# Dealing adjacent weight rows to partitions, so that expert weights come in 4 KB packets

## The chip, the core and the metric

The kernel runs on one core of a Trainium2 chip. The time is device microseconds of one execution. Before the change three runs gave 1325.62, 1323.4 and 1325.61 us, median 1325.61. The engines are TensorE (PE, matmuls; PEld are its weight loads), VectorE (DVE), ScalarE (ACT), GpSimd (POOL) and SyncE (SP), which here issues every DMA.

## The reference

One block of a diffusion backbone on 256 latent tokens with 256 context tokens, D = 2048, all in float32. Cut to what matters:

```python
mods_x = split((silu(c) @ w_mod + b_mod), 6)          # shift, scale, gate for attention; shift, scale, gate for ffn
nx = modulated_norm(h_x, attn_norm, sa_x, sca_x)       # rmsnorm * (1 + scale) + shift
... = split(nx @ w_in)                                 # latent attention (8 heads) and gated short convolution
h_new = h_x + ga_x * merge_head_groups(o_mla, o_conv)  # o @ w_out
# mixture of experts: 32 experts of width 256, 4 of them for each token, and a shared expert of width 512
idx, w = route(xf, w_router, bias)
g, u = xf @ w_exp_gate[e], xf @ w_exp_up[e]            # (2048, 256) each, for every expert e
routed = sum_e (silu(g) * u * comb[:, e]) @ w_exp_down[e]      # (256, 2048)
shared = (silu(xf @ w_sh_gate) * (xf @ w_sh_up)) @ w_sh_down
out = rmsnorm(h_new + gf_x * (routed + shared), final_norm)
```

where xf is the modulated norm of h_new with ffn_norm, shift sf_x and scale scf_x. A product over D sums 2048 rows, and the order of the rows is free as long as activations and weights agree on it.

## The kernel before, in words

The program is written out by hand, one instruction stream for each engine with semaphores between them. The order of work is the order of the code; only buffers that come free set when a DMA starts.

*Start (0 to about 83 us).* SyncE loads constants, x and ctx, then the first slices of w_mod (2 MB each), then w_in and more of w_mod. PE multiplies silu(c) with w_mod in groups of 512 columns. Groups 0 to 7 go through PE. For groups 8 and on VectorE accumulates w_mod rows (L1239) into the tile `part`, and PE only sums over partitions: `mod_sum_cols` (L508) takes 128 columns of `part` as weights and a column of ones as the moving side, four times for each group. It leaves one modulation value per partition. Groups 8 to 15 are the shift and scale of the ffn; they become `modT` and `amul2`.

*Attention and convolution (to about 574 us)*, then the ffn norm: VectorE (L1456) and ScalarE (L1082) write normalised rows `xh` from `xres`, one half of the tokens each, in four chunks of 512 columns. PE transposes them (L778) into `hT`, and router and shared expert follow.

*Experts.* `ring` holds the weights of one pair of experts: gate and up in four quarters of the 2048 rows (`gu`), down in two tiles. `load_quarter` (L404) issues four DMAs of 512 KB for a quarter, `load_down` (L411) one for each slice of 512 columns and each expert. Row 128 c + p of a weight lies on partition p, so a packet, the piece contiguous in HBM and in SBUF, has 256 numbers (1 KB) for gate and up and 512 (2 KB) for down. A pair has passes of 64 tokens for each expert. In a pass PE multiplies the gathered tokens with gate and up (L485, 64 matmuls as the trace counts them), gathers the tokens of the next pass with bf16 matmuls from three parts of `xh`, applies down, and scatters with `pickT`; VectorE adds (L1619). PE frees quarter q for SyncE with `gu_used[q]`, down with `down_used[n]`. There are 16 pairs and 17 passes. Code before and after the loop over pairs is separate code, and a pass that may be left out stands before each pass.

Of the kernel before, what the change touches and what calls it, by code (L numbers as in the profile page):

```python
# [9 lines left out]
ACT = mybir.ActivationFunctionType  # L10
# [5 lines left out]
P = 128  # L16
D = 2048
T = 256
KC = D // P
# [5 lines left out]
NE, NG, FF = 32, 4, 256  # L25
# [15 lines left out]
V_AN, V_QN, V_KN, V_CW, V_OM, V_OC, V_FN = 0, 16, 20, 22, 46, 54, 62  # L41
# [32 lines left out]
def block_kernel(nc, x, c, ctx_in, c_ctx, w_mod, b_mod, attn_norm, w_in, q_a_norm, w_q_b, kv_a_norm, w_kv_b,  # L74
                 conv_w, o_norm_mla, o_norm_conv, w_out, ffn_norm, w_router, router_bias,
                 w_exp_gate, w_exp_up, w_exp_down, w_sh_gate, w_sh_up, w_sh_down, final_norm, consts, out):
    with ExitStack() as stack:
        def sb(name, shape, dt=F32):
            return stack.enter_context(nc.sbuf_tensor(name, shape, dt))

        def sem(name):
            return stack.enter_context(nc.semaphore(name))


        xres = sb("xres", [P, 2, D])
# [6 lines left out]
        part = sb("part", [P, 2, 512])  # L92
        modT = sb("modT", [P, 96, 2])
# [8 lines left out]
        csil = sb("csil", [32, P])  # L102
        vecT = sb("vecT", [P, NVEC])
        bT = sb("bT", [P, 96])
        amul = sb("amul", [P, KC, 2])
        amul2 = sb("amul2", [P, KC])
        stat = sb("stat", [P, 16])
        wr = sb("wr", [P, KC, NE])
# [22 lines left out]
        xh = slot[3].rearrange("p (t d) -> p t d", t=2)  # L131

        gu = ring[:, 0:16384].rearrange("p (q u g k n) -> p q u g k n", q=4, u=2, g=2, k=4)
        down = [slot[4 + u].rearrange("p (k n) -> p k n", k=2) for u in range(2)]
# [85 lines left out]
        down_in = [sem(f"down_in{n}") for n in range(4)]  # L220
        down_used = [sem(f"down_used{n}") for n in range(4)]
# [3 lines left out]
        gu_full, silu_done, act_ready, actT_full, actT_out, dn_full, ye_out, sc_full, y_add = (  # L225
            sem("gu_full"), sem("silu_done"), sem("act_ready"), sem("actT_full"), sem("actT_out"), sem("dn_full"),
            sem("ye_out"), sem("sc_full"), sem("y_add"))
        mean_sq, root, mean_wide, root_wide = sem("mean_sq"), sem("root"), sem("mean_wide"), sem("root_wide")
        fin_h, fin_sq, fin_gain, fin_dve, fin_act, stored = (sem("fin_h"), sem("fin_sq"), sem("fin_gain"),
                                                             sem("fin_dve"), sem("fin_act"), sem("stored"))  # L230
# [5 lines left out]
        wq = w_q_b[0].rearrange("(c p) n -> p c n", p=P)  # L236
        wkv = w_kv_b[0].rearrange("(c p) n -> p c n", p=P)
        wo = w_out[0].rearrange("(c p) n -> p c n", p=P)
        wg = w_exp_gate[0].rearrange("e (c p) n -> p e c n", p=P)
        wu = w_exp_up[0].rearrange("e (c p) n -> p e c n", p=P)  # L240
        wd = w_exp_down[0].rearrange("e (c p) n -> p e c n", p=P)
        sg = w_sh_gate[0].rearrange("(c p) n -> p c n", p=P)
        su = w_sh_up[0].rearrange("(c p) n -> p c n", p=P)
        sd = w_sh_down[0].rearrange("(c p) n -> p c n", p=P)

        def k_of(s, k):
            return slot[s].rearrange("p (k n) -> p k n", k=k)

        FIRST = 0

# [17 lines left out]


        SH_SLOT = (0, 1, 2, 0, 4, 5)  # L270
        SH_USE = (11, 10, 11, 12, 1, 2)

        block = stack.enter_context(nc.Block())

# [2 lines left out]
        def _(sp):  # L277
# [77 lines left out]
            sp.dma_start(wr[:, :, :], w_router[0].rearrange("(c p) n -> p c n", p=P)).then_inc(router_in, 16)  # L355
            sp.dma_start(rb[:, :], router_bias.to_broadcast([P, NE])).then_inc(router_in, 16)


# [36 lines left out]
            sp.dma_start(k_of(2, KC), sg[:, :, FF:2 * FF]).then_inc(w_full[2], 16)  # L395
# [3 lines left out]
            sp.dma_start(k_of(0, KC), sg[:, :, 0:FF]).then_inc(w_full[0], 16)  # L399
            sp.dma_start(k_of(5, 2), sd[:, 2:4, :]).then_inc(w_full[5], 16)  # L400
            sp.wait_ge(sh_gate, 2)
            sp.dma_start(k_of(0, KC), su[:, :, FF:2 * FF]).then_inc(w_full[0], 16)


            def load_quarter(i, q):
                for u in range(2):
                    for g, src in ((0, wg), (1, wu)):
                        sp.dma_start(gu[:, q, u, g, :, :].rearrange("p k n -> p (k n)").rearrange("p (k n) -> p k n", k=4),
                                     src[:, bass.ds(2 * i + u, 1), 4 * q:4 * q + 4, :]
                                     .rearrange("p a c n -> p (a c) n")).then_inc(gu_in[q], 16)  # L410
# [12 lines left out]
            sp.wait_ge(sh_gate, 4)  # L423
            load_quarter(0, 2)
            sp.wait_ge(sh_down, 8)
            for n in range(4):
# [4 lines left out]
            for n in range(4):  # L431
                load_down(0, n, 1)
            with sp.Fori(1, NE // 2) as i:
                for q in range(4):
                    sp.wait_ge(gu_used[q], i)
                    load_quarter(i, q)
                for n in range(4):
# [45 lines left out]
        def _(pe):  # L483
            def mm(o, l, r, start, stop):
                return nc.tensor.matmul(o, l, r, start=start, stop=stop)  # L485
# [364 lines left out]
            def pair_pass(i, t, last, ahead=True):  # L850
# [27 lines left out]
                def scatter(n):  # L878
                    pe.wait_ge(ye_out, 4 * t + (n + 1))
                    for h in range(2):  # L880
                        m = 2 * n + h
                        pe.wait_ge(y_add, 8 * t + (16 + max(m - 1, 0)))
                        ins = mm(ps[:, 6 + h, :], pickT[:, 128 * h:128 * h + 128], ye[:, 512 * n:512 * n + 512], True, True)
                        if n < 3 and h == 0 and last:
                            ins.then_inc(down_used[n + 1], 1)
                    ins.then_inc(sc_full, 1)

                for n in range(4):
                    pe.wait_ge(down_in[n], 32 * i + 32)
                    if n >= 2:  # L890
                        pe.wait_ge(ye_out, 4 * t + (n - 1))
                    for k in range(2):
                        for u in range(2):
                            ins = mm(ps[64 * u:64 * u + 64, 4 + n % 2, :], actT[:, k, 64 * u:64 * u + 64],
                                     down[u][:, k, 512 * n:512 * n + 512], k == 0, k == 1)
                            if n == 1 and k == u == 0 and last:
                                ins.then_inc(down_used[0], 1)
                    ins.then_inc(dn_full, 1)
                    if n == 0:
                        pe.wait_ge(pickT_out, t + 1)  # L900
                    else:
                        scatter(n - 1)
# [23 lines left out]
        def _(sc):  # L926
# [251 lines left out]
        def _(ve):  # L1178
# [141 lines left out]
            with ve.Fori(0, 4) as i:  # L1320
# [21 lines left out]
                for m in range(2):  # L1342
# [4 lines left out]
            steps[0] += 4 * LINKS  # L1347

            ve.wait_ge(modT_done, 16)
            link(V.tensor_tensor(modT[:, 48:80, 0:1], modT[:, 48:80, 0:1], bT[:, 48:80].unsqueeze(2), ALU.add))  # L1350
            V.scalar_tensor_tensor(out=amul2[:, :].rearrange("p (c a) -> p c a", a=1), in0=modT[:, 64:80, 0:1], scalar=1.0,
                                   in1=vecT[:, V_FN:V_FN + KC].rearrange("p (c a) -> p c a", a=1),
                                   op0=ALU.add, op1=ALU.mult).then_inc(mods_ready, 1)


# [97 lines left out]
            ve.wait_ge(root, roots[0])  # L1453
            ve.wait_ge(mods_ready, 1)
            for n in range(4):
                V.tensor_scalar(xh[:, 0, 512 * n:512 * n + 512], xres[:, 0, 512 * n:512 * n + 512], stat[:, 10:11], None,  # L1456
                                ALU.mult).then_inc(xh_ready, 1)
# [236 lines left out]
```

## Time and profile before

| | |
|---|---|
| median of three runs | 1325.61 us |
| span of the profiled execution, first to last instruction | 1322.1 us |
| PE busy | 1222.6 us |
| DVE busy | 517.6 us |
| ACT busy | 227.0 us |
| DMA | 379.59 MB, mean 287 GB/s |
| packets | 276337, of them under 2 KB 182864 |

The profile is of one execution, whose own time is given by its span alone; the runs beside it are timed from outside. Busy shares are averages over stages. Idle time of an engine counts only where the chain that ended last runs through it.

### The profile page before, as it was taken

Reading aid. Unit: us, or ns where it says so; the run is one execution under the profiler, and the core shown is the slowest. Engines: PE = TensorE matmul, PEld = TensorE weight load, DVE = VectorE, ACT = ScalarE, POOL = GpSimd, SP = SyncE. Lnnn points to the kernel's source line nnn. Section 1 sums busy time; section 2 is a strip of 40 time slices with the busy share of each in tenths; the row PEclk is TensorE's granted clock in tenths of the full one; section 3 lists DMA queues with packets and bytes.
Section 4 is the critical chain, followed back from the end, with each engine's and each line's share of the span. In section 5 each row is a group of like instructions: output and inputs, shape, how many; then the busy total and the mean of one; then the engine's idle time right before and its main releaser. Section 6 shows DMA issues by size and latency. Waiting matters only on the chain.

```text
span 1322.1 us, 16803 instructions
## 1 busy us (share of the span) xinstructions
PE 1222.6 (92%) x6125; PEld 655.8 (50%) x6126; DVE 517.6 (39%) x1058; ACT 227.0 (17%) x482; POOL 8.7 (1%) x13
## 2 busy tenths in 40 slices
PE   2789999999999899989979999999999999999974
PEld 0435588888744544457834444444334444444421
DVE  1200487656267588542532222222223332222215
ACT  4210200000125400040011111111111111111103
POOL 0000000000000000000000000000000000000001
PEclk9989999999999999989989999999999999999988
DMA  9999989996574499763549999945999999999951
GB/s 341 345 354 335 315 297 366 350 326 219 163 278 141 151 343 387 274 243 128 181 145 361 344 344 345 347 156 162 348 348 346 350 349 357 343 345 346 347 198 63
DMA packets 276337, 379.59 MB, mean 287 GB/s; under 512 B 12674, under 2 KB 182864, under 8 KB 274640
## 3 DMA queue, kind: packets, MB, share of 16 engines
q1 hardware_dynamic: 276304, 379.14, 84.1%
q8 instruction: 22, 0.36, 0.1%
q14 instruction: 11, 0.09, 0.0%
HBM read 377.01 MB, written 2.10 MB: 287 GB/s over the span
## 4 chain that ended last, share of the span: by engine, by line
PE 88%; DVE 3%; DMA 3%; issue 2%; SPq 2%; ACT 1%; POOL 0%; POOLq 0%; DVEq 0%; ACTq 0%
PE ps L485 85%; DMA ring<-in_w_mod 3%; DVE nreg L1619 1%; PE ps L855 1%; SPq L311 1%; PE ps L778 0%; SPq L303 0%; DVE tiny L1386 0%; PE ps L555 0%; DVE nreg L1623 0%; PE ps L730 0%; PE ps L872 0%; ACT nreg L928 0%; PE ps L500 0%; ACT nreg L1049 0%
## 5 line engine op out<-in xcount | busy, mean ns | idle before, releaser
L485 PE MATMUL ps<-nreg,ring 128*128 128x256 f32 (+1 forms) x1280 | 301.0, 395 | 10.2 <-ACT nreg L928 5.8
L485 PEld LDWEIGHTS ps<-nreg,ring 128*128 128x128 f32 x1280 | 244.0, 192 | 63.9 <-issue 21.8
L485 PE MATMUL ps<-ring,nreg 128*64 128x512 f32 x1088 | 241.2, 602 | 0.0
L1239 DVE SCALAR_TENSOR_TENSOR part<-ring,csT,part 128x512 f32<-128x512 f32 x240 | 180.4, 752 | 9.2
L1619 DVE TENSOR_TENSOR nreg<-nreg,ps 128x512 f32<-128x512 f32 x136 | 87.4, 684 | 176.2 <-PE ps L485 176.2
L485 PEld LDWEIGHTS ps<-ring,nreg 128*64 128x64 f32 x1088 | 77.5, 139 | 151.9 <-issue 151.9
L485 PE MATMUL ps<-nreg,conv 128*128 128x512 f32 x272 | 134.9, 618 | 13.5 <-DVE nreg L1619 13.5
L485 PE MATMUL ps<-ring,conv 128*64 128x512 f32 x544 | 128.0, 602 | 0.5 <-ACT conv L928 0.5
L485 PE MATMUL ps<-ring 128*128 128x512 f32 x256 | 110.8, 592 | 0.0
L485 PEld LDWEIGHTS ps<-nreg,conv 128*128 128x128 f32 x272 | 46.0, 189 | 101.5 <-DVE nreg L1619 60.2
L485 PE MATMUL ps<-pick,qnT 128*128 128x128 bf16 x544 | 93.2, 220 | 1.1 <-issue 0.6
L928 ACT ACTIVATE nreg<-ps 128x512 f32<-128x512 f32 (+1 forms) x104 | 57.7, 555 | 208.6 <-PE ps L485 195.7
L485 PE MATMUL ps<-pick,kq 128*128 128x128 bf16 x544 | 92.9, 219 | 0.0
L485 PE MATMUL ps<-pick,hb 128*128 128x128 bf16 x544 | 92.9, 219 | 0.0
L485 PEld LDWEIGHTS ps<-ring 128*128 128x128 f32 x256 | 48.6, 190 | 60.4 <-issue 60.3
L1611 DVE TENSOR_TENSOR conv<-ps,conv 128x256 f32<-128x256 f32 x17 | 7.2, 425 | 178.9 <-ACT conv L1124 178.9
L485 PEld LDWEIGHTS ps<-ring,conv 128*64 128x64 f32 x544 | 34.5, 136 | 76.7 <-issue 74.3
L1600 DVE TENSOR_SCALAR nreg<-ps,amul,modT 128x128 f32<-128x128 f32 x136 | 46.5, 405 | 63.9 <-PE ps L485 63.9
L1116 ACT ACTIVATE nreg<-ps,modT,amul 128x128 f32<-128x128 f32 x136 | 51.2, 456 | 66.0 <-PE ps L485 66.0
L485 PEld LDWEIGHTS ps<-pick,qnT 128*128 128x128 bf16 x544 | 53.1, 98 | 18.5 <-issue 14.2
L928 ACT ACTIVATE conv<-ps 128x256 f32<-128x256 f32 x42 | 16.2, 385 | 228.2 <-PE ps L485 139.4
L485 PE MATMUL ps<-ring,csT 128*32 128x512 f32 x256 | 33.7, 655 | 23.3 <-DMA ring<-in_w_mod 23.3
(193 smaller groups left out, 753.1 us busy)
## 6 DMA issues: line engine op xcount, KB each, us to landing
ring<-in_w_mod SPq DMA_DIRECT2D x88, 1024.0 KB, 9.4
ring<-in_w_exp_gate SPq DMA_DIRECT2D x128, 512.0 KB, 8.2
ring<-in_w_exp_up SPq DMA_DIRECT2D x128, 512.0 KB, 8.6
ring<-in_w_exp_down SPq DMA_DIRECT2D x128, 512.0 KB, 8.6
ring<-in_w_in SPq DMA_DIRECT2D x15, 2048.0 KB, 11.9
ring<-in_w_out SPq DMA_DIRECT2D x8, 2048.0 KB, 10.9
ring<-in_w_mod SPq DMA_DIRECT2D x4, 2048.0 KB, 19.8
ring<-in_w_sh_up SPq DMA_DIRECT2D x2, 2048.0 KB, 10.2
```

The lines of the kernel that those rows point to most:

```text
L311: sp.dma_start(slots_[q], wm[:, 4 * q:4 * q + 4, bass.ds(g * 512, 512)]).then_inc(m_full[q], 16)
L485: return nc.tensor.matmul(o, l, r, start=start, stop=stop)
L855: ins = nc.tensor.transpose(ps[:, 3, 128 * j:128 * j + 128], pickw[:, j, :], ident)
L928: return nc.scalar.activation(o, i_, ACT.Copy)
L1116: ins = nc.scalar.activation(xg[:, k, :], ps[:, b % 2, 128 * j:128 * j + 128], ACT.Identity, bias=modT[:, 3 * KC + k, 0:1], scale=amul2[:, ...
L1239: ins = V.scalar_tensor_tensor(out=acc, in0=w, scalar=scale, in1=acc, op0=ALU.mult, op1=ALU.add)
L1600: ins = V.tensor_scalar(xg[:, k, :], ps[:, b % 2, 128 * j:128 * j + 128], amul2[:, k:k + 1], modT[:, 3 * KC + k, 0:1], ALU.mult, ALU.add)
L1611: V.tensor_tensor(act[:, 1, :], ps[:, 2, FF:2 * FF], act[:, 0, :], ALU.mult).then_inc(act_ready, 1)
L1619: V.tensor_tensor(yacc[:, h, cols], yacc[:, h, cols], ps[:, 6 + h, :], ALU.add).then_inc(y_add, 1)
```

## The change

Rows of gate and up are dealt anew: partition p takes rows 512 q + 4 p + j for quarter q and j = 0 to 3. Its four rows lie side by side in HBM, 4 KB in one packet. The router's weights are dealt likewise, and the shared expert's gate and up too; since these are loaded by halves of their columns, their packets stay 1 KB, and each load becomes four DMAs. Down is loaded in two halves of 1024 columns (4 KB packets) instead of four slices, with two semaphores instead of four.

The activations have to be dealt alike. `xh` is written so that its chunk 4 q + j holds columns 512 q + 4 c + j: the two norm writers read `xres` with a step of four elements and write without gaps. The modulation sums take every fourth column of `part`. Bias and gain in that order are loaded by three new DMAs with 16-byte pieces.

```diff
+            for at, src in ((bT2[:, 0:KC], b_mod[0, 3 * D:4 * D]), (bT2[:, KC:2 * KC], b_mod[0, 4 * D:5 * D]),
+                            (fnT[:, :], ffn_norm[0])):
+                sp.dma_start(at.rearrange("p (q j) -> p q j", q=4), src.rearrange("(q p j) -> p q j", q=4, j=4))\
+                  .then_inc(cols_in, 16)
             sp.wait_ge(mod_rows, 1)
...
-        wg = w_exp_gate[0].rearrange("e (c p) n -> p e c n", p=P)
+        wg = w_exp_gate[0].rearrange("e (q p j) n -> p e q (j n)", q=4, j=4)
-        sg = w_sh_gate[0].rearrange("(c p) n -> p c n", p=P)
+        sg = w_sh_gate[0].rearrange("(q p j) n -> p q j n", q=4, j=4)
...
+        def by_row(v, n):
+            return v.rearrange("p (j c) -> p j c", c=n)
+        def by_col(v):
+            return v.rearrange("p (c j) -> p j c", j=4)
...
-            sp.dma_start(k_of(1, KC), su[:, :, 0:FF]).then_inc(w_full[1], 16)
+            def load_shared(s, src, half):
+                for q in range(4):
+                    sp.dma_start(k_of(s, KC)[:, 4 * q:4 * q + 4, :], src[:, q, :, FF * half:FF * half + FF])\
+                      .then_inc(w_full[s], 16)
+            load_shared(1, su, 0)
...
-                sp.dma_start(down[u][:, :, 512 * n:512 * n + 512],
-                             wd[:, bass.ds(2 * i + u, 1), :, 512 * n:512 * n + 512]
+                sp.dma_start(down[u][:, :, 1024 * n:1024 * n + 1024],
+                             wd[:, bass.ds(2 * i + u, 1), :, 1024 * n:1024 * n + 1024]
...
-                    ins = mm(ps[:, 5, j:j + 1], part[:, b, 128 * j:128 * j + 128], ones[:, 0:1], True, True)
+                    ins = mm(ps[:, 5, j:j + 1], part[:, b, :].rearrange("p (c j) -> p j c", j=4)[:, j, :], ones[:, 0:1],
+                             True, True)
...
-                        if n < 3 and h == 0 and last:
-                            ins.then_inc(down_used[n + 1], 1)
+                        if n in (0, 2) and h == 0 and last:
+                            ins.then_inc(down_used[n // 2], 1)
...
-                            if n == 1 and k == u == 0 and last:
-                                ins.then_inc(down_used[0], 1)
...
-                nc.scalar.activation(xh[:, 1, 512 * n:512 * n + 512], xres[:, 1, 512 * n:512 * n + 512], ACT.Identity,
-                                     scale=stat[:, 11:12]).then_inc(xh_act, 1)
+                nc.scalar.activation(by_row(xh[:, 1, 512 * n:512 * n + 512], 128), by_col(xres[:, 1, 512 * n:512 * n + 512]),
+                                     ACT.Identity, scale=stat[:, 11:12]).then_inc(xh_act, 1)
```

VectorE's norm writer (L1456) changes in the same way, and `modT` and `amul2` are built from `bT2` and `fnT` behind a wait on `cols_in`.

On SyncE, at the start of the program, this stands before:

```order
L291 DMA ring<-in_ctx 128x2x2048
L295 DMA ring<-in_w_mod 128x8x512 x4
L300 DMA ring<-in_w_in 128x16x256 x2
L302 DMA ring<-in_w_in 128x16x256
L303 DMA kq<-in_w_in 128x16x64
```

and this after the change (`bT` is the order's name for bT2):

```order
L300 DMA ring<-in_ctx 128x2x2048
L304 DMA ring<-in_w_mod 128x8x512 x4
L309 DMA bT<-in_b_mod 128x4x4 x2
L309 DMA fnT<-in_ffn_norm 128x4x4
L313 DMA ring<-in_w_in 128x16x256 x2
L315 DMA ring<-in_w_in 128x16x256
L316 DMA kq<-in_w_in 128x16x64
```

Three DMAs of 16-byte pieces have come in between w_mod and w_in.

On SyncE, at the end of one turn of the loop over pairs, before (L414 is the line of `load_down`; ISA is a wait; `128x2x512 x2` is one slice for two experts):

```order
L408 DMA ring<-in_w_exp_gate 128x4x256
L408 DMA ring<-in_w_exp_up 128x4x256
L414 DMA ring<-in_w_exp_down 128x2x512 x2
L414 ISA
L414 DMA ring<-in_w_exp_down 128x2x512
```

and after:

```order
L427 DMA ring<-in_w_exp_gate 128x1024
L427 DMA ring<-in_w_exp_up 128x1024
L432 DMA ring<-in_w_exp_down 128x2x1024 x2
L432 ISA
L432 DMA ring<-in_w_exp_down 128x2x1024
```

The order of gate, up and down is unchanged; a piece of gate and up is one row of 1024 numbers, and down goes out in four DMAs of a turn and not eight.

## Rows read from the trace of the kernel before

**Rows 1.** The cores: span, and mean granted clock of TensorE.
```profile
core 0: 1322.1 us, clock 0.980
```

**Rows 2.** The page: busy us (share, instructions); DMA queue (packets, MB, share).
```profile
PE 1222.6 (92%) x6125; PEld 655.8 (50%) x6126; DVE 517.6 (39%) x1058; ACT 227.0 (17%) x482; POOL 8.7 (1%) x13
...
q1 hardware_dynamic: 276304, 379.14, 84.1%
```

**Rows 3.** Waits of PE, whole span: releaser, us in total, times, longest.
```profile
PE ps L485 <- DMA ring<-in_w_mod: 23.3, 7, 15.2
...
PE ps L485 <- DMA ring<-in_w_in: 1.9, 1, 1.9
```

**Rows 4.** Chain of waits, end of the start: start us, us, what.
```profile
73.52 9.74 DMA ring<-in_w_mod
```

**Rows 5.** Waits of PE from 700 to 1300 us, all of them.
```profile
PE ps L485 <- DVE nreg L1619: 12.5, 16, 0.8
PE ps L855 <- issue: 6.0, 2, 5.8
PE ps L872 <- DVE conv L1611: 0.9, 1, 0.9
PE ps L485 <- ACT conv L928: 0.5, 1, 0.5
```

**Rows 6.** Chain of waits, first matmuls of two successive passes.
```profile
904.87 16.67 PE ps L485 x112
...
941.04 16.67 PE ps L485 x112
```

**Rows 7.** Stretches of one pass: busy, clock, DMA share, GB/s last.
```profile
953.00:957.00 4.00, 4.00 (x49) 2.58 (x46) 0.42 (x1) 0.97 (x3) 0.00 (x0) 1.00 1.10 348
...
973.00:977.00 4.00, 3.12 (x9) 0.93 (x7) 1.59 (x3) 0.00 (x0) 0.00 (x0) 1.00 1.06 388
```

**Rows 8.** Waits of SyncE's queue, 904 to 1270 us.
```profile
SPq L408 <- PE ps L485: 110.5, 20, 42.1
```

**Rows 9.** Chain of waits, the two longest pieces of issue.
```profile
678.95 6.83 issue
...
1265.79 5.82 issue
```

**Rows 10.** DMA queues, 1265 to 1272 us: packets, MB, share.
```profile
q1 hardware_dynamic: 1097, 2.10, 81.4%
q8 instruction: 1, 0.02, 1.0%
```

**Rows 11.** Stretches at the second stall, columns as in rows 7.
```profile
1269.00:1270.00 1.00, 0.00 (x0) 0.00 (x0) 0.00 (x0) 0.00 (x0) 0.00 (x0) 1.00 0.98 373
1270.00:1271.00 1.00, 0.00 (x0) 0.00 (x0) 0.00 (x0) 0.00 (x0) 0.00 (x0) 0.52 0.39 135
```

**Rows 12.** Timeline of PE, gate and up matmuls of two passes.
```profile
940.97 13.96 PE L485 MATMUL ps<-ring,nreg 128*64 128x512 f32 x64
...
1272.22 16.24 PE L485 MATMUL ps<-ring,nreg 128*64 128x512 f32 x64
```

**Rows 13.** Stretches at the start, columns as in rows 7.
```profile
52.00:56.00 4.00, 4.00 (x20) 3.54 (x19) 0.00 (x0) 0.00 (x0) 0.00 (x0) 1.00 1.10 348
56.00:60.00 4.00, 2.11 (x9) 1.18 (x8) 0.00 (x0) 0.00 (x0) 0.00 (x0) 1.00 1.05 206
```

**Rows 14.** Timeline: weight loads of one column sum.
```profile
188.00 1.08 PEld L485 LDWEIGHTS ps<-cst,part 128*128 128x128 f32 x8
```

**Rows 15.** Timeline: norm writers and transposes.
```profile
577.92 2.56 ACT L1082 ACTIVATE ring<-xres,stat 128x512 f32<-128x512 f32 x4 [1.21 <-POOL stat L467]
577.92 1.68 DVE L1456 TENSOR_SCALAR ring<-xres,stat 128x512 f32<-128x512 f32 x4 [0.82 <-POOL stat L467]
...
578.78 6.21 PE L778 MATMUL ps<-cst,ring 128*128 128x128 f32 x32 [4.83 <-ACT ring L1082]
```

**Rows 16.** Timeline: down loads of the loop's last turn, third scatter.
```profile
1254.49 8.77 SPq L414 DMA_DIRECT2D ring<-in_w_exp_down  x8
...
1261.04 1.98 PE L485 MATMUL ps<-nreg,conv 128*128 128x512 f32 x4
```

More of the change, by code:

```diff
@@ L104, in block_kernel @@
         bT = sb("bT", [P, 96])
+        bT2 = sb("bT2", [P, 2 * KC])
+        fnT = sb("fnT", [P, KC])
         amul = sb("amul", [P, KC, 2])
@@ L219, in block_kernel @@
         gu_used = [sem(f"gu_used{q}") for q in range(4)]
-        down_in = [sem(f"down_in{n}") for n in range(4)]
-        down_used = [sem(f"down_used{n}") for n in range(4)]
+        down_in = [sem(f"down_in{n}") for n in range(2)]
+        down_used = [sem(f"down_used{n}") for n in range(2)]
         pick_ready, pickw_ready, gx_full, gx_act, gx_dve, pickT_full, pickT_out = (
@@ L227, in block_kernel @@
             sem("ye_out"), sem("sc_full"), sem("y_add"))
+        cols_in = sem("cols_in")
         mean_sq, root, mean_wide, root_wide = sem("mean_sq"), sem("root"), sem("mean_wide"), sem("root_wide")
@@ L238, in block_kernel @@
         wo = w_out[0].rearrange("(c p) n -> p c n", p=P)
-        wg = w_exp_gate[0].rearrange("e (c p) n -> p e c n", p=P)
-        wu = w_exp_up[0].rearrange("e (c p) n -> p e c n", p=P)
+        wg = w_exp_gate[0].rearrange("e (q p j) n -> p e q (j n)", q=4, j=4)
+        wu = w_exp_up[0].rearrange("e (q p j) n -> p e q (j n)", q=4, j=4)
         wd = w_exp_down[0].rearrange("e (c p) n -> p e c n", p=P)
-        sg = w_sh_gate[0].rearrange("(c p) n -> p c n", p=P)
-        su = w_sh_up[0].rearrange("(c p) n -> p c n", p=P)
+        sg = w_sh_gate[0].rearrange("(q p j) n -> p q j n", q=4, j=4)
+        su = w_sh_up[0].rearrange("(q p j) n -> p q j n", q=4, j=4)
         sd = w_sh_down[0].rearrange("(c p) n -> p c n", p=P)
@@ L270, in block_kernel @@
         SH_SLOT = (0, 1, 2, 0, 4, 5)
-        SH_USE = (11, 10, 11, 12, 1, 2)
+        SH_USE = (14, 13, 14, 18, 1, 2)
         block = stack.enter_context(nc.Block())
@@ L354, in _ @@
             sp.dma_start(k_of(2, 2), wkv).then_inc(w_full[2], 16)
-            sp.dma_start(wr[:, :, :], w_router[0].rearrange("(c p) n -> p c n", p=P)).then_inc(router_in, 16)
+            sp.dma_start(wr[:, :, :].rearrange("p (q j) n -> p q (j n)", q=4),
+                         w_router[0].rearrange("(q p j) n -> p q (j n)", q=4, j=4)).then_inc(router_in, 16)
             sp.dma_start(rb[:, :], router_bias.to_broadcast([P, NE])).then_inc(router_in, 16)
@@ L392, in _ @@
             sp.wait_ge(wo_full, 3)
-            sp.dma_start(k_of(1, KC), su[:, :, 0:FF]).then_inc(w_full[1], 16)
+            def load_shared(s, src, half):
[3 more added lines that the diff above has]
+            load_shared(1, su, 0)
             sp.wait_ge(wo_half, 4)
-            sp.dma_start(k_of(2, KC), sg[:, :, FF:2 * FF]).then_inc(w_full[2], 16)
+            load_shared(2, sg, 1)
             sp.wait_ge(acc_done, 16 * 16)
@@ L398, in _ @@
             sp.wait_ge(wo_full, 4)
-            sp.dma_start(k_of(0, KC), sg[:, :, 0:FF]).then_inc(w_full[0], 16)
+            load_shared(0, sg, 0)
             sp.dma_start(k_of(5, 2), sd[:, 2:4, :]).then_inc(w_full[5], 16)
             sp.wait_ge(sh_gate, 2)
-            sp.dma_start(k_of(0, KC), su[:, :, FF:2 * FF]).then_inc(w_full[0], 16)
+            load_shared(0, su, 1)
             def load_quarter(i, q):
@@ L407, in load_quarter @@
                     for g, src in ((0, wg), (1, wu)):
-                        sp.dma_start(gu[:, q, u, g, :, :].rearrange("p k n -> p (k n)").rearrange("p (k n) -> p k n", k=4),
-                                     src[:, bass.ds(2 * i + u, 1), 4 * q:4 * q + 4, :]
-                                     .rearrange("p a c n -> p (a c) n")).then_inc(gu_in[q], 16)
+                        sp.dma_start(gu[:, q, u, g, :, :].rearrange("p k n -> p (k n)"),
+                                     src[:, bass.ds(2 * i + u, 1), q, :].rearrange("p a x -> p (a x)")).then_inc(gu_in[q], 16)
             def load_down(i, n, u):
-                sp.dma_start(down[u][:, :, 512 * n:512 * n + 512],
-                             wd[:, bass.ds(2 * i + u, 1), :, 512 * n:512 * n + 512]
+                sp.dma_start(down[u][:, :, 1024 * n:1024 * n + 1024],
+                             wd[:, bass.ds(2 * i + u, 1), :, 1024 * n:1024 * n + 1024]
                              .rearrange("p a c n -> p (a c) n")).then_inc(down_in[n], 16)
@@ L425, in _ @@
             sp.wait_ge(sh_down, 8)
-            for n in range(4):
+            for n in range(2):
                 load_down(0, n, 0)
@@ L430, in _ @@
             sp.wait_ge(sh_down, 16)
-            for n in range(4):
+            for n in range(2):
                 load_down(0, n, 1)
@@ L436, in _ @@
                     load_quarter(i, q)
-                for n in range(4):
+                for n in range(2):
                     sp.wait_ge(down_used[n], i)
@@ L883, in scatter @@
                         ins = mm(ps[:, 6 + h, :], pickT[:, 128 * h:128 * h + 128], ye[:, 512 * n:512 * n + 512], True, True)
-                        if n < 3 and h == 0 and last:
-                            ins.then_inc(down_used[n + 1], 1)
+                        if n in (0, 2) and h == 0 and last:
+                            ins.then_inc(down_used[n // 2], 1)
                     ins.then_inc(sc_full, 1)
                 for n in range(4):
-                    pe.wait_ge(down_in[n], 32 * i + 32)
+                    if n % 2 == 0:
+                        pe.wait_ge(down_in[n // 2], 32 * i + 32)
                     if n >= 2:
@@ L1349, in _ @@
             ve.wait_ge(modT_done, 16)
-            link(V.tensor_tensor(modT[:, 48:80, 0:1], modT[:, 48:80, 0:1], bT[:, 48:80].unsqueeze(2), ALU.add))
+            ve.wait_ge(cols_in, 48)
+            link(V.tensor_tensor(modT[:, 48:80, 0:1], modT[:, 48:80, 0:1], bT2[:, :].unsqueeze(2), ALU.add))
             V.scalar_tensor_tensor(out=amul2[:, :].rearrange("p (c a) -> p c a", a=1), in0=modT[:, 64:80, 0:1], scalar=1.0,
-                                   in1=vecT[:, V_FN:V_FN + KC].rearrange("p (c a) -> p c a", a=1),
+                                   in1=fnT[:, :].rearrange("p (c a) -> p c a", a=1),
                                    op0=ALU.add, op1=ALU.mult).then_inc(mods_ready, 1)
@@ L1455, in _ @@
             for n in range(4):
-                V.tensor_scalar(xh[:, 0, 512 * n:512 * n + 512], xres[:, 0, 512 * n:512 * n + 512], stat[:, 10:11], None,
-                                ALU.mult).then_inc(xh_ready, 1)
+                V.tensor_scalar(by_row(xh[:, 0, 512 * n:512 * n + 512], 128), by_col(xres[:, 0, 512 * n:512 * n + 512]),
+                                stat[:, 10:11], None, ALU.mult).then_inc(xh_ready, 1)
             gate_out(OUT_GROUP + 3)
```

## The prediction

> **What bounds the kernel now.** I began with the cores and the busy shares: one core, a mean granted clock of 0.980 [rows 1], TensorE (PE) busy 92% of 1322.1 us and the DMA queue 84% [rows 2]. Both are near full, so either could be the limit, and the list of TensorE's waits has to decide. It says [rows 3] that PE waited 25.2 us for weights by DMA (23.3 for w_mod, 1.9 for w_in). The chain of waits, in order of time, has the last of it at 73.52 to 83.3 us [rows 4]; from there the chain runs through PE. In the stretch 700 to 1300 us, where the expert weights are used, no DMA ends a wait of PE: the list has four rows [rows 5], 12.5 us behind VectorE's adds, 6.0 us of "issue" and crumbs.
>
> The chain also gives the beat of one expert pair, 904.87 to 941.04 us, 36.2 us [rows 6]. The bytes of one pair are 24 loads of 512 KB, 12.6 MB: 8.4 MB of gate and up in 1 KB packets at 348 GB/s, 24.1 us, and 4.2 MB of down in 2 KB packets at 388, 10.8 us [rows 7], together 34.9. So DMA fills its beat almost as PE does, but the one who waits is SyncE, 110.5 us for PE's release of gate and up buffers [rows 8], and not PE. A quarter is loaded when PE frees it and read one beat later. In this stretch faster packets shorten transfers that nobody waits for, and I cost the gain at nothing. PE's 36.2 us are the cover; transfers would have to get slower, not faster, to show.
>
> **Where DMA is on the path.** Two places are left. First the start, up to 83 us. Secondly, two stalls of PE that the chain calls "issue", at 678.95 us (6.83 us) and 1265.79 us (5.82 us) [rows 9]. Both stand where PE goes from one piece of program to another, into the pair loop and out of it. The DMA listing of the second has one packet of the instruction queue beside 2.10 MB of weights [rows 10]. Weights flow at 373 GB/s until 1270, at 135 in the next microsecond, and PE goes on at 1271.6 [rows 9, 11]. I read this as the program's fetch standing behind queued weight packets, which is an inference. After the stall the granted clock is 0.52 and less, TensorE's lower level (1.2 GHz) [rows 11], and the 64 gate and up matmuls of the last pass take 16.24 us against 13.96 in a pass at full clock [rows 12]: 2.3 us more.
>
> **The change part by part.**
> 1. *Start.* Three DMAs go in front of the first w_in load, 512 packets each of 16 bytes, 1536 in all. DMA is the limit there, so they are paid in full. The nearest row is the load of wkr, 2048 packets of 256 bytes: from 56 to 60 us DMA moved 206 GB/s where it had moved 348 before [rows 13]. 4 x 142 = 568 KB are lost, 1.6 us, and its own 0.52 MB cost 1.5 us more. For each packet that is 0.8 ns lost, or 1.5 ns with the payload: 1536 x 0.8 = 1.2 us, 1536 x 1.5 = 2.3 us. I take 1.8; ends 0 (if they slip into slack) and +5 (if 16 bytes are far worse than 256). The Trainium skill, "DMA: Bandwidth & Descriptors", Specifications, says that a transfer below 512 B is a read-modify-write; the wkr row has such packets too and would already carry that price.
> 2. *Column sums of the modulation.* Eight groups (n = 8 to 15) now give PE its weights from part with a step of four elements, 16 bytes. Before, the 8 weight loads of one sum take 1.08 us [rows 14], and eight sums 8.6 us, on PE's chain and hidden by nothing. No row shows a PE read with such a step. If it costs nothing, 0; if each load takes twice its time, +8.6 us. A gain is excluded, since the instructions are as many. I take 0: these fp32 loads need 0.13 us for 128 columns, a slow pace already, and fetching may not be what sets it. The upper end is rival B.
> 3. *Normalised rows.* Eight instructions now read xres with a 16-byte step. VectorE's four take 1.68 us and ScalarE's four 2.56 us, and PE, which waited 4.83 us for the first, then needs 6.21 us for 32 transposes [rows 15]. Only the first pair is ahead of PE; the others come every 0.64 us while PE takes 1.55 us for each. VectorE's 0.42 us may grow to ScalarE's 0.64 without being seen. If ScalarE's doubles, PE starts 0.6 to 0.7 us later. I take +0.4, ends 0 and +1.4 (both engines also hand back the transposes, later by as much).
> 4. *Shared expert, router, cols_in.* Four loads for one, with the same 1 KB packets: SyncE has nine more issues, among waits for PE. PE waited for none of these loads [rows 3, 5], nor for the router's, whose packets get longer. The wait on cols_in stands at the end of the convolution stage, far behind its loads. 0 for all.
> 5. *Expert loads.* I take 400 GB/s for 4 KB packets, an estimate a little above the 388 of 2 KB. Two releases of down stand for four. SyncE's first down load now waits for the first scatter; in the last turn SyncE comes to down only at 1254.49 us, about when that scatter is under way. The second waits for the third scatter, which starts at 1261.04 [rows 16], as the last load does now. 0 on the path.
> 6. *The two stalls.* At the second, the last 2.1 MB of down are released at 1262 us, 1 us into the third scatter. With 1 us to start and 5.2 us at 400 GB/s they end at 1268.3, where now the flow ends near 1270.4 [rows 11]. The stall shrinks by 2.1 us, from 5.8 to 3.7. The clock may then stay up or not: half of 2.3, 1.1 us. At the first stall the 2.1 MB of down in flight should end 1 us sooner (0.6 us by rate alone, 388 to 400 and a quicker start): 1.0. Together -4.2 us, ends 0 and -7.
>
> Sum: 1.8 + 0 + 0.4 + 0 + 0 - 4.2 = -2.0 us. The profiled execution has a span of 1322.1 us and the runs' median is 1325.61, so 3.5 us lie around the span or between executions. 1325.6 - 2.0 = 1323.6 us.
>
> **Rivals.**
> A, the forecast: no large term, 1323.6 us, own range 1320.5 to 1327. Chance 0.48.
> B, strided weight loads cost. Each of the 64 load records takes up to twice its time, +4 to +8.6 us: 1328 to 1332. For it: nothing covers them, the matmul beside each has one column. Against: the loads are slow already. It decides from +0.07 us a load (4.5 us, which outweighs the stalls). Chance 0.22. The Trainium skill, "SBUF — State Buffer", in "Door 1: The DMA port swizzle", speaks for it: reads want at least two hits in each 16-byte line, and a step of four fp32 has one. By that rule the loads, and the eight instructions of point 3, slow down. No row of before shows such a read, and the page gives no size.
> C, the 16-byte packets cost 5 us: 1325.6 + 5 + 0.4 - 4.2 = 1327 us. For it, they are 16 times smaller than wkr's; against, they carry next to no bytes. Chance 0.08.
> D, both stalls shrink by their upper end and the clock is kept: -7, so 1325.6 + 1.2 - 7 = 1320 us. For it are the rates in the stall; against, down's last half is still released as late. Chance 0.18.
> E, DMA sets the beat after all, and 16 pairs gain 1 us or more, to 1308 us. Against it is the list of waits, with not one DMA row. Chance 0.04.
>
> **How the numbers follow.** 0.2% is 2.65 us, about what runs of this kernel can tell from no change (its three runs span 2.2 us). Faster, below 1322.9: 0.15 of A, all of D and E, 0.37. Slower, above 1328.3: 0.01 of A, 0.2 of B and 0.04 of C, 0.25. Same: 0.38. The range for 8 in 10 reaches from 1319, a little beyond D, to 1330, the middle of B.
>
> **What would show it.** Right: the beat of a pair stays 36.2 us while DMA moves 400 GB/s in it, with pauses between; the last wait for w_mod, at 73 to 83 us, ends 1 to 2 us later; the 8 loads on part still take 1.08 us; the stall near 1266 us is 2 us shorter. Wrong: another beat than 36.2 us (E, or contention that I have not seen), 2 us for 8 loads on part (B), a start later by 4 us or more (C), or stalls as long as before although the transfers end sooner, which would refute my reading of them.

## The result, and the profile after

The changed kernel is slower: 1335.49 us median (1334.11 to 1336.61, 4 runs) against 1325.06 (1323.4 to 1325.62, 4 runs), a ratio of 1.0082 with a 95% interval of 1.0067 to 1.0096. The forecast was 1323.6, range 1319 to 1330; the time lies above that range, and above the 1328 to 1332 us of rival B too. The cost of rival B came true (6.9 us, of 4 to 8.6), but it is not the whole. The profiled execution has a span of 1334.3 us, 12.2 more than the one of before. It is among the slower ones of its four, and some of the 12.2 us is where the clock happened to fall.

The page first: busy time, and the DMA queue (packets, MB, share).

```profile
span 1334.3 us, 16601 instructions
...
PE 1231.7 (92%) x6125; PEld 664.2 (50%) x6126; DVE 518.2 (39%) x1058; ACT 228.3 (17%) x482; POOL 8.7 (1%) x13
...
q1 hardware_dynamic: 160832, 379.16, 78.3%
```

Beside [rows 2], the bytes are the same and the packets are 160832 instead of 276304; the queue's share fell from 84.1 to 78.3%. So the change does what it says to DMA. PE has as many instructions and 9.1 us more of them, PEld 8.4 us more.

The chain of waits (start us, us, what) gives the account by places. These are the end of the start, the convolution stage, the first stall and two successive passes.

```profile
73.48 11.22 DMA ring<-in_w_mod
84.74 1.98 PE ps L503 x8
...
88.50 15.25 PE ps L503 x64
...
162.72 236.46 PE ps L503 x1052
...
688.53 7.43 issue
...
915.83 16.67 PE ps L503 x112
...
951.99 16.67 PE ps L503 x112
...
1276.88 7.32 issue
```

| stretch | before | after | more |
|---|---|---|---|
| to the end of the last w_mod wait | 83.3 | 84.7 | 1.4 |
| from there to the convolution stage | 75.5 | 78.0 | 2.5 |
| convolution stage, unbroken on PE | 229.5 | 236.5 | 6.9 |
| from its end to the output projection | 68.6 | 66.8 | -1.8 |
| from there to the router's matmuls (the norm lies in it) | 128.1 | 128.6 | 0.5 |
| first stall | 6.83 [rows 9] | 7.43 | 0.6 |
| from its end to the second stall | 580.0 | 580.9 | 0.9 |
| of this, beat of a pair | 36.17 [rows 6] | 36.16 | 0 |
| second stall | 5.82 [rows 9] | 7.32 | 1.5 |
| behind it | 50.5 | 50.1 | -0.4 |

From the router's matmuls to the first stall it is 94.0 us in either. Leaving out the beat, the lines add up to the 12.2 us but for rounding. The second line is the clock: the 8 matmuls behind the last wait take 1.98 us instead of 1.11 and the next 64 take 15.25 instead of 14.09, since PE's clock is at its lower level there (0.50 from 84 to 88 us in the table of stretches, 1.00 before). The line of -1.8 us is the clock as well: the same 203 matmuls, at a mean granted clock of 0.95 before and 0.97 after. Of the 0.9 us between the stalls, 112 matmuls behind the first stall account for all (19.20 us against 18.33), again at a low clock. The beat is the main thing that the change is about, and it has not moved. DMA in the pairs is as foreseen, as these stretches of the pass at 915.83 show (columns as in rows 7).

```profile
918.00:922.00 4.00, 4.00 (x22) 1.39 (x20) 1.83 (x8) 0.00 (x0) 0.00 (x0) 1.00 0.30 100
922.00:926.00 4.00, 4.00 (x20) 1.29 (x18) 0.00 (x0) 0.00 (x0) 0.00 (x0) 1.00 1.02 398
926.00:930.00 4.00, 4.00 (x25) 1.36 (x22) 0.00 (x0) 0.24 (x1) 0.00 (x0) 1.00 1.01 408
```

Gate and up flow at 398 to 408 GB/s where [rows 7] show 348, and there is now a pause (100 GB/s) in which nothing has been released. PE is as busy as ever. SyncE's wait for PE's releases (line, releaser, us, times, longest) has grown:

```profile
SPq L432 <- PE ps L503: 150.1, 20, 8.4
SPq L427 <- PE ps L503: 141.0, 40, 42.1
```

That is 291 us over 915 to 1281 us. Before, [rows 8] had 110.5 for gate and up, and down had 34.4. The growth is some 14 us a beat, and the transfers got only some 3 us shorter (12.6 MB at about 400 GB/s, an estimate, against 34.9 us). The rest was spent in issuing: before, once a few loads were under way, an issue of gate or up took 1.2 to 1.7 us, and in this pass each takes 0.33 to 0.39 (timelines of SyncE's queue). Both times stand in the same place, off PE's path.

The convolution stage grows by the weight loads of the column sums. Timeline of PEld, one sum:

```profile
191.93 1.94 PEld L503 LDWEIGHTS ps<-cst,part 128*128 128x128 f32 x8
```

1.94 us stands against 1.08 in [rows 14], 0.86 more, eight times: 6.9 us, the whole growth of the stage. Of one load the median is 329 ns and was 192 (loads overlap, so eight take less than eight times that).

### The profile page after: what moved, and what is told of

The parts are those of the page before. It is cut to its first block, busy times and chain, and to the rows that moved or that the text cites. A ratio compares the mean times of both kernels' runs of the same rounds, so it can differ in the third digit from the quotient of the medians.

```text
span 1334.3 us, 16601 instructions
## 1 busy us (share of the span) xinstructions
PE 1231.7 (92%) x6125; PEld 664.2 (50%) x6126; DVE 518.2 (39%) x1058; ACT 228.3 (17%) x482; POOL 8.7 (1%) x13
## 3 DMA queue, kind: packets, MB, share of 16 engines
q1 hardware_dynamic: 160832, 379.16, 78.3%
## 4 chain that ended last, share of the span: by engine, by line
PE 88%; DMA 3%; DVE 3%; issue 2%; ACT 2%; SPq 1%; POOL 0%; POOLq 0%; DVEq 0%; ACTq 0%
PE ps L503 85%; DMA ring<-in_w_mod 3%; DVE nreg L1638 1%; PE ps L574 1%; PE ps L874 1%; SPq L324 1%; SPq L316 0%; DVE tiny L1405 0%; DVE nreg L1642 0%; ACT ring L1100 0%; PE ps L518 0%; PE ps L749 0%; PE ps L891 0%; ACT nreg L946 0%; ACT nreg L1067 0%
```

## The experiments

### The strided weight loads, undone

```diff
-                    ins = mm(ps[:, 5, j:j + 1], part[:, b, :].rearrange("p (c j) -> p j c", j=4)[:, j, :], ones[:, 0:1],
-                             True, True)
+                    ins = mm(ps[:, 5, j:j + 1], part[:, b, 128 * j:128 * j + 128], ones[:, 0:1], True, True)
```

> The changed kernel, with the column sums of the modulation taken from part in contiguous pieces of 128 columns again (this leaves out the dealing of the modulation values, so they stand in the wrong order; no amount of work changes). In the changed kernel the median weight load on part is 329 ns against 192 before, and the chain of PE from 162.72 to 399.21 us is 236.5 us long against 229.5. Theory (strided weight loads are the main cost): loads back to 192 ns, that stretch back to 229.5 us, and the run 6.9 us faster than the changed kernel, about 1328.5 us. Rival (the stretch is longer for another reason, for instance packets of other sizes beside it): loads short, but the stretch stays near 236 us and the run near 1335 us.

1328.07 us (10 runs), ratio to before 1.0018 (1.0006 to 1.0029). The loads on `part` (min/median/max ns of a load) and the chain:

```profile
L503 PEld LDWEIGHTS ps<-cst,part x68: 186/192/192, 191.9 to 590.5; 128*128 128x128 f32 x68
```
```profile
162.70 229.53 PE ps L503 x1052
```

The stage is back at 229.53 us and the run 7.4 us faster than the changed kernel. The start stayed as in the changed kernel (162.70), so nothing there helped. Of the 10.4 us this is about two thirds, shown by taking it out. The firm figure is the 6.93 us of the stage; the ten times reach from 1324.62 to 1329.53 us, so the 7.4 is good to a microsecond or two.

### A step of two elements

On the kernel before, the loads take every second column:

```diff
-                    ins = mm(ps[:, 5, j:j + 1], part[:, b, 128 * j:128 * j + 128], ones[:, 0:1], True, True)
+                    ins = mm(ps[:, 5, j:j + 1], part[:, b, 256 * (j // 2):256 * (j // 2) + 256].rearrange("p (c j) -> p j c", j=2)[:, j % 2, :],
+                             ones[:, 0:1], True, True)
```

> The kernel before, with the weight loads of the column sums taking every second column of part (8 bytes apart) where the changed kernel takes every fourth (16 bytes). Order of the modulation values is not kept. Theory (a load is slowed once each element lies in a 16-byte line of its own): at two elements to a line the loads stay at 192 ns and the time at 1325 us. Rival (any step above one element slows the read): loads of 230 to 330 ns, and +2 to +7 us.

```profile
L485 PEld LDWEIGHTS ps<-cst,part x68: 186/196/197, 188.2 to 588.3; 128*128 128x128 f32 x68
```

196 ns and not 192, 1324.89 us, and the stage 229.87 us. A step of 8 bytes costs 2%, one of 16 bytes 71%. The Trainium skill, "SBUF — State Buffer", in "Door 1: The DMA port swizzle", says that at least two hits in each 16-byte line are needed for full bandwidth. The trace agrees (196 ns with two hits in a line, 329 ns with one), and it adds the size. Steps of 12 bytes and above 16 were not tried on PE, so that the 16-byte line is the reason, and not the length of the step, is the page's word and not shown.

### The 16-byte pieces, loaded later

```diff
-            for at, src in ((bT2[:, 0:KC], b_mod[0, 3 * D:4 * D]), (bT2[:, KC:2 * KC], b_mod[0, 4 * D:5 * D]),
...
             sp.wait_ge(mod_rows, 1)
...
+            for at, src in ((bT2[:, 0:KC], b_mod[0, 3 * D:4 * D]), (bT2[:, KC:2 * KC], b_mod[0, 4 * D:5 * D]),
...
             for s in range(2):
                 sp.wait_ge(conv_full, 20 + 2 * s)
```

> The changed kernel, with the three DMAs of 16-byte pieces issued behind the convolution loop instead of in front of the first w_in load. Theory (they delay the start by DMA time alone, 1.4 us, and the rest of the 3.9 us at the start is the granted clock, which falls at other moments): the last w_mod wait ends at 83.3 us again instead of 84.7, the run is 1.4 us faster than the changed kernel, give or take 2 us of clock, so 1332 to 1335 us. Rival (the pieces cost the whole 3.9 us, in SyncE's queue, where their issue took 11 us): 3.9 us faster, 1331.5 us, in every run.

The first place is in front of the first w_in load, the second behind the convolution loop. 1333.31 us (4 runs), ratio 1.0065 (1.0048 to 1.0082), 2.2 us below the changed kernel; the two intervals overlap (1.0067 to 1.0096 there), so this difference is not clear of noise. The chain at the end of the start:

```profile
73.69 9.56 DMA ring<-in_w_mod
83.29 1.11 PE ps L503 x8
...
85.72 14.09 PE ps L503 x64
...
158.90 236.46 PE ps L503 x1052
```

The wait ends at 83.25 us again, and the 2.5 us of slow clock behind it are gone too, in this execution. What the pieces do is seen in the timeline of SyncE's queue in the changed kernel:

```profile
24.73 8.29 SPq L309 DMA_DIRECT2D bT<-in_b_mod  x2
33.06 2.67 SPq L309 DMA_DIRECT2D fnT<-in_ffn_norm  x1
35.77 4.54 SPq L313 DMA_DIRECT2D ring<-in_w_in  x2
```

Their issue holds SyncE for 11 us, but the w_in loads behind them, issued at 35.77 us and not 30.5, still arrive in time to keep DMA busy. Hence 1.4 us of delay and not 11. The same three DMAs in this run, issued behind the convolution loop, take 1.4 us:

```profile
309.32 0.93 SPq L360 DMA_DIRECT2D bT<-in_b_mod  x2
310.30 0.51 SPq L360 DMA_DIRECT2D fnT<-in_ffn_norm  x1
```

DMA is as busy at either place (386 and 389 GB/s), but at the start four loads of 2 MB have been issued just ahead of them and here four of 1 MB. So the 11 us are not the price of the pieces; that they are the time in which a full queue drains is my reading.

The 2.2 us of the medians lie between my expectation (1.4) and the rival's 3.9. The other profiles part the two costs. With the pieces in front the last w_mod wait ends at 84.70, 84.51 and 84.03 us (the changed kernel, the run with contiguous column sums, and the first run of the next section), without them at 83.21 to 83.54 in nine profiles: 0.5 to 1.5 us are theirs. The clock is not tied to them. In the third of these three it is up again by 80 us and the convolution stage starts at 159.63 us, 0.8 later than before; and in the packets-only run below, without any such pieces, it is low at this place, and the stage starts at 162.00 us.

### The norm writers: stride on the other side, and alone

First, in the changed kernel, reading without gaps and writing with a step of 128 elements:

```diff
+        def to_rows(v):
+            return v.rearrange("p (j c) -> p c j", j=4)
...
+        def as_cols(v):
+            return v.rearrange("p (c j) -> p c j", j=4)
...
-                nc.scalar.activation(by_row(xh[:, 1, 512 * n:512 * n + 512], 128), by_col(xres[:, 1, 512 * n:512 * n + 512]),
+                nc.scalar.activation(to_rows(xh[:, 1, 512 * n:512 * n + 512]), as_cols(xres[:, 1, 512 * n:512 * n + 512]),
```

> The changed kernel, with the eight norm instructions reading xres without gaps and writing xh with a step of 128 elements, where the changed kernel reads with a step of four and writes without gaps; the result is the same tile. In the changed kernel ScalarE's four take 4.59 us against 2.56 before. Theory (the strided read is what costs): ScalarE back to 2.6 us for four, and the transposes start 0.5 us sooner. Rival (any stride on either side costs as much): 4.6 us again, or more, since the step is 512 bytes.

Then, in the kernel before, the dealt form alone (the same two views as in the change).

> The kernel before, with the eight norm instructions alone in their dealt form (reading xres with a step of four). The router then meets rows in the wrong order, so the number of passes in the expert stage may differ, and only the norm stage is to be read. Theory: ScalarE's four take 4.6 us, VectorE's four 2.5 us, and the stretch from the first of them to the router's matmuls grows by 0.5 to 0.6 us over the 7.0 us of before (577.92 to 584.92). Rival (the cost was in the changed kernel's surroundings): 7.0 us again.

Timeline of the three, ScalarE, VectorE and PE. The changed kernel:

```profile
586.95 4.59 ACT L1100 ACTIVATE ring<-xres,stat 128x512 f32<-128x512 f32 x4 [1.21 <-POOL stat L485]
586.95 2.47 DVE L1475 TENSOR_SCALAR ring<-xres,stat 128x512 f32<-128x512 f32 x4 [0.81 <-POOL stat L485]
...
594.49 1.93 PE L503 MATMUL ps<-nreg,wr 128*32 128x256 f32 x32
```

With the step on the writing side:

```profile
585.67 4.46 ACT L1106 ACTIVATE ring<-xres,stat 128x512 f32<-128x512 f32 x4 [1.21 <-POOL stat L491]
585.67 2.59 DVE L1481 TENSOR_SCALAR ring<-xres,stat 128x512 f32<-128x512 f32 x4 [0.81 <-POOL stat L491]
```

In the kernel before, alone:

```profile
576.44 4.58 ACT L1082 ACTIVATE ring<-xres,stat 128x512 f32<-128x512 f32 x4 [1.21 <-POOL stat L467]
...
584.02 1.93 PE L485 MATMUL ps<-nreg,wr 128*32 128x256 f32 x32
```

Against 2.56 and 1.68 us in [rows 15] both engines lose, ScalarE 80% and VectorE about 47%. My theory that only the read costs fell: the form that writes with a step of 512 bytes costs as much. Its two views also run over four elements at a time and not over 128, and no run parts this from the step. The stretch to the router's matmuls is 7.58 us alone and 7.54 in the changed kernel, where it was 7.0, so +0.5 us; close to the prediction's 0.4. The single times, 1332.88 and 1322.56 us, say no more than that nothing large hangs on it.

### The packets alone

In the kernel before, only the expert loads are changed (gate and up in rows of 4 KB, down in halves); the activations are not dealt to match.

```diff
-        wg = w_exp_gate[0].rearrange("e (c p) n -> p e c n", p=P)
+        wg = w_exp_gate[0].rearrange("e (q p j) n -> p e q (j n)", q=4, j=4)
...
-                sp.dma_start(down[u][:, :, 512 * n:512 * n + 512],
+                sp.dma_start(down[u][:, :, 1024 * n:1024 * n + 1024],
```

> The kernel before, with every expert load in 4 KB packets (gate, up and down as in the changed kernel), and nothing else of the change: activations are not dealt, so gate and up meet rows in the wrong order. Theory (the expert stage is bound by PE, so packets alone are worth nothing but what they do to the two stalls): beat of a pair 36.2 us, stalls of about 7.3 and 6.7 us as with down in halves, the run within 2 us of before, 1323 to 1326 us. Rival (larger packets do help or hurt PE in the pairs): a beat that differs by more than 0.1 us, the run over 2 us away.

1326.06 us (11 runs), ratio 1.0004 (0.9995 to 1.0013): no difference that can be measured. Its chain:

```profile
680.51 7.47 issue
...
762.38 16.67 PE ps L484 x112
...
798.52 16.67 PE ps L484 x112
...
1267.75 6.61 issue
```

The beat is 36.14 us. The gain that the packets might bring, 348 to 400 GB/s, is off the critical path. The two stalls are longer than before (7.47 and 6.61 us). To part down from gate and up, down alone in halves (the second edit above without the first, with two semaphores as in the change):

> The kernel before, with only down changed: two halves of 1024 columns with 4 KB packets and two semaphores, the rest as before. In the changed kernel the second stall is 6.7 to 7.3 us against 5.8 before, though down is the only load in flight there. Theory (down's first half is released later and so more of it is still on its way): the stall is 6.7 us or more here too. Rival (it comes from the packets of gate and up, or from chance): 5.8 us. Beat of a pair 36.2 us in either case.

Its stalls are 7.33 and 6.79 us. The three profiles with down in slices and weights in flight have 6.58 to 6.83 and 5.80 to 5.84 us, the seven with down in halves 7.19 to 7.47 and 6.61 to 7.32, so it is down's halves that lengthen them, by 0.4 to 0.9 us at the first and mostly 0.8 to 1.0 at the second; the 7.32 of the changed kernel is the longest of its kind. The first half waits for the first scatter, and then comes in pieces of 1 MB; which of the two does it is not shown. The one time was 1322.37 us, below the median of before: in its profile the stretch between the convolution stage and the output projection takes 66.7 us and not 68.6 (388.37 to 455.05 us, 388.33 to 456.94 before), with the same instructions, and more of the slow clock falls into the longer stalls themselves (the matmuls behind the first take 17.92 us, 18.33 before). One run cannot price the stalls.

### The two stalls

This is the kernel before with down loads kept out of the way:

```diff
             sp.wait_ge(sh_down, 16)
+            sp.wait_ge(pickT_full, 1)
             for n in range(4):
                 load_down(0, n, 1)
-            with sp.Fori(1, NE // 2) as i:
+            with sp.Fori(1, NE // 2 - 1) as i:
...
+            i = NE // 2 - 1
+            for q in range(4):
+                sp.wait_ge(gu_used[q], i)
+                load_quarter(i, q)
+            sp.wait_ge(gu_used[0], NE // 2)
+            for n in range(4):
+                sp.wait_ge(down_used[n], i)
+                for u in range(2):
+                    load_down(i, n, u)
```

> The kernel before, with down loads moved out of the way of the two stalls: the second expert's down of pair 0 is issued only once PE has started the pair code, and the down of the last pair only once PE has used the first gate and up quarter of that pair. Same work, same packets. Theory (the program's fetch stands behind queued weight packets): the stalls of 6.8 and 5.8 us shrink to 3 to 4 us each, the clock mostly stays up behind them, and the run is 5 to 9 us faster than before, 1316 to 1320 us. Rival (the fetch takes that long by itself, or is asked for late): stalls of 5.8 us or more again, and 1325 us.

1317.13 us (4 runs, 1316.72 to 1317.98), ratio 0.9949 (0.9933 to 0.9966): 7.2 us faster than before, and the fastest of all kernels here. Its chain:

```profile
679.07 4.17 issue
...
1263.42 3.07 issue
1266.94 15.55 PE ps L494 x64
```

6.83 and 5.82 us have become 4.17 and 3.07, with no weights in flight; the stretches of both show 0 to 16 GB/s. That is 5.4 us. The matmuls behind them are 1.0 us faster too, 17.97 and 15.55 us against 18.33 and 16.20 before, since less of them falls under the low clock; the two profiled spans differ by 6.0 us in all. So weights in flight lengthen the stalls, and the reading in the prediction holds that far: the program's fetch stands behind weight packets. But 3 to 4 us stay without any.

The packet of the instruction queue shows where the time goes. In slices of 0.1 us its place in each stall can be seen:

| profile | stalls | packet, us after PE stopped | PE goes on, us after the packet |
|---|---|---|---|
| before | 6.83, 5.82 | 4.2, 3.1 | 2.6, 2.7 |
| down in halves | 7.33, 6.79 | 4.7, 4.1 | 2.6, 2.7 |
| changed kernel | 7.43, 7.32 | 4.8, 4.8 | 2.6, 2.5 |
| this run | 4.17, 3.07 | 1.6, 0.5 | 2.6, 2.6 |

The time behind the packet is 2.5 to 2.9 us in all 24 stalls of the twelve profiles, whatever flows; weights in flight lengthen only the time up to it, by 2.6 us at either stall here. PE does not wait for the flow to end: at the second stall of before the packet passes at 1268.9 us, while DMA moves 403 GB/s and goes on at 373 in the next microsecond [rows 11].

### All mends together, and one that did not mend

VectorE deals while it accumulates, so that PE's loads are contiguous again, and the 16-byte pieces are late:

```diff
-                acc = part[:, b, :]
+                acc = by_row(part[:, b, :], 128) if dealt else part[:, b, :]
...
+                        if dealt:
+                            w = by_col(w)
...
```

> The changed kernel with VectorE dealing the columns while it accumulates and with the 16-byte pieces loaded behind the convolution loop, stalls as they are. Loads on part 192 ns; the accumulating instructions, 752 ns before, stay below 900 ns if VectorE is slowed by the step as little as its norm writer (0.42 to 0.62 us), and their pace stays off PE's path: PE's stretch 229.5 us, the run 1326 us (1335.5 - 6.9 - 2.2). Rival (a strided read slows VectorE's two-operand form as well and the accumulation becomes the bound in the convolution stage): over 1 us an instruction, PE waiting for VectorE there, and 1330 us or more.

1333.28 us (4 runs), ratio 1.0078 (1.0061 to 1.0095), where I had expected 1326. That is the 1333.31 of the run with late pieces alone, so taking the step away from PE brought nothing. The rival was right. VectorE's group in the convolution stage (busy us, mean ns), and the head of the chain there, 158 to 210 us:

```profile
L1258 DVE SCALAR_TENSOR_TENSOR part<-ring,csT,part 128x512 f32<-128x512 f32 x135 | 148.6, 1101 | 4.7
```
```profile
by line: DVE part L1258 62.4%; issue 8.0%; PE ps L503 6.5%; DVE kq L1214 6.5%; DVE qkv L1328 2.6%; DVE part L1255 2.5%; DVE conv L1356 2.2%; DVE conv L1348 1.4%; DVE qkv L1313 1.4%; DVE qkv L1334 1.4%; DVE kq L1209 1.2%; ACT kq L1004 1.2%; 
```

The mean of 1101 ns has some undealt instructions in it; from 167 to 202 us, where all are dealt, it is 1144. That instead of 752 ns makes VectorE the bound at the start of the stage, where PE had hidden it. The cost went from one engine to another.

The same with the late down loads:

> The changed kernel with all mends together: VectorE deals the columns while it accumulates (it reads w_mod with a step of four and writes part in contiguous pieces), so that PE's loads are contiguous; the 16-byte pieces are loaded behind the convolution loop; down loads stay out of the way of the two stalls as in the run on the kernel before. By the theory of the stalls: 1317 to 1321 us, faster than before, with nothing of it owed to 4 KB packets. Rival (stalls unchanged): 1326 us.

1325.68 us (8 runs), ratio 1.0016 (1.0005 to 1.0028). Its stalls are 4.00 and 3.04 us. It is 7.6 us below the run above, as on the kernel before (7.2), so the mend of the stalls works on either; but the whole missed its 1317 to 1321 by VectorE's loss.

## Why the prediction was wrong

1. *What bounds the kernel: right.* No DMA ends a wait of PE in the pairs, and faster packets are worth nothing there (ratio 1.0004 for the packets alone).
2. *The column sums: the first of two steps that failed.* The prediction took 0 between ends of 0 and +8.6 us, "these fp32 loads need 0.13 us for 128 columns, a slow pace already, and fetching may not be what sets it". They took +6.9 us, 1.94 us for 8 instead of 1.08. Pace told nothing of slack: no row showed how much of it was fetching, and the one rule at hand spoke for the cost. I had it as rival B with a chance of 0.22. With the right value the sum would have been 1330.5, still 5 us short: the other step is in point 5.
3. *The start: size about right, clock missed.* 1.8 us taken, 1.4, 1.3 and 0.8 measured at the last w_mod wait in three profiles. In the profiled execution a low clock made 2.5 us more of it; the medians put the whole at 2.2, with noise of that size. The rows of before show this place at full clock, and the prediction said nothing of the clock here.
4. *The norm: right*, 0.4 taken, 0.5 measured. VectorE's 0.42 us grew to 0.62, as allowed for, and ScalarE's 0.64 to 1.15, just short of the doubling that I had priced at 0.6 to 0.7.
5. *The stalls: the second step that failed, and about as large.* I took -4.2 us. They grew by 0.6 and 1.5 us, and the slower clock behind them cost 0.5 more, where 1.1 of gain stood in the 4.2. The prediction let the stall end 1.2 us behind the end of the flow, and the flow end 2.1 us sooner, at 400 GB/s after a start of 1 us. Neither came. The flow did not end sooner: the run with down in halves kept 344 to 426 GB/s for five microseconds around PE's stop, and still 1.68 MB came behind the stop (1.78 before). In the changed kernel it was slower, 164 to 336 GB/s at 1274 to 1279 us, and faded at 1281, 4 us into the stall:

```profile
1274.00:1275.00 1.00, 0.22 (x2) 0.11 (x1) 0.85 (x2) 0.00 (x0) 0.00 (x0) 1.00 0.69 164
...
1278.00:1279.00 1.00, 0.00 (x0) 0.00 (x0) 0.20 (x1) 0.00 (x0) 0.00 (x0) 1.00 0.95 336
...
1280.00:1281.00 1.00, 0.00 (x0) 0.00 (x0) 0.00 (x0) 0.00 (x0) 0.00 (x0) 1.00 0.52 205
```

   (Stretches of 1 us, changed kernel.) And the end of the flow is not what PE waits for: PE goes on 2.5 to 2.9 us behind the instruction packet, which passed 3.1 us after PE's stop before the change, 4.1 with down in halves and 4.8 in the changed kernel. That the fetch stands behind weights was right; its time was tied to the wrong event. Why the packet passes later with down in halves is open.

The account in medians: 10.4 us = 7.4 for the strided loads (taken out), 2.2 for the 16-byte pieces (taken out, not clear of noise), and 0.8 left for the norm and the stalls. That is less than those two show in the profile (0.5 and 2.1), by no more than the clock moves one stretch from one execution to the next (66.8 or 68.6 us from the convolution stage to the output projection). Only the first of the three is firm.

## What to carry to other kernels

Dealing a weight's rows to get longer packets has to be paid by whoever makes the activations match, and a step of 16 bytes in fp32 is not free on any of the three engines; look for that bill first, above all where the strided operand is a weight load that nothing covers. Before wanting faster transfers, see who waits: if SyncE waits for releases and no DMA ends a wait of PE, the packets are worth nothing. And where the chain shows "issue" at the door of a loop with weights in flight, move those weights: here that gave 7.2 us with no change of work, while 3 to 4 us of each stall stayed.

## What the runs showed that I had not expected

- The step's price for each element read: PE 137 ns for 128 (1.07 ns), ScalarE about 0.5 us for 512 (1.0 ns), VectorE 392 ns for 512 in the two-operand form (0.77 ns) and about 0.2 us for 512 in the one-operand form (0.4 ns). On PE's path the loads overlap, and 0.86 us for eight is 108 ns a load. With a step of 8 bytes PE pays 4 ns for 128.
- Small DMAs can look dear at their issue: 1536 pieces of 16 bytes behind 8 MB of loads held SyncE for 11 us and delayed the start by 0.8 to 1.4 us; behind 4 MB the same issue took 1.4 us.
- PE's clock can add 2.5 us at one place in one execution and not in another: the convolution stage started at 162.7 us in two profiles with the pieces in front and at 159.6 in the third, and at 158.8 to 159.0 in most without them and 162.0 in one.
- An instruction packet is followed by 2.5 to 2.9 us before PE goes on, with or without weights in flight.
